# Seven block products instead of eight in all four gate and up pairs of two feed-forward stages

## What is computed

```python
def swiglu(x, w_gate, w_up, w_down):
    return (jax.nn.silu(x @ w_gate) * (x @ w_up)) @ w_down

    h = h + 0.5 * rmsnorm_2(swiglu(u, ff1_w_gate[i], ff1_w_up[i], ff1_w_down[i]), ff1_post_g[i])
    ...
    h = h + 0.5 * rmsnorm_2(swiglu(u, ff2_w_gate[i], ff2_w_up[i], ff2_w_down[i]), ff2_post_g[i])
```

## Time and profile before

| | us |
|---|---|
| median of 3 runs | 2850.26 |
| the runs | 2849.7 to 2850.55 |
| the profiled execution | 2850.18 |
| its span, first to last instruction | 2848.4 |
| mean granted TensorE clock | 0.998 |

### The profile page before, as it was taken

The page is one execution under the profiler, slowest core; times in us unless marked ns, Lnnn a source line. Parts: engine busy times, 40 slices in busy tenths (PEclk is TensorE's granted clock), DMA queues, the critical chain, the costliest instruction groups (busy, mean ns, idle before and its releaser), DMA issues.

```text
span 2848.4 us, 33903 instructions
## 1 busy us (share of the span) xinstructions
PE 2821.0 (99%) x13298; PEld 2358.2 (83%) x13298; DVE 2001.3 (70%) x2140; ACT 1379.1 (48%) x1544; POOL 14.4 (1%) x20
## 2 busy tenths in 40 slices
PE   9999999999999999999999999999999999999998
PEld 7888888888898788888888888888778888888887
DVE  5469756455565777777777777786777777777785
ACT  5344545454544544444444455655544444444464
POOL 0000000000000000000000000000000000000000
PEclk9999999999999999999999999999999999999999
DMA  7556355555546555555555558543655655555554
GB/s 239 194 165 197 111 186 180 193 180 176 168 148 201 187 197 189 195 195 195 198 192 191 192 170 270 173 151 129 221 178 188 206 191 191 194 195 197 195 177 155
DMA packets 276001, 530.60 MB, mean 186 GB/s; under 512 B 8769, under 2 KB 32465, under 8 KB 275393
## 3 DMA queue, kind: packets, MB, share of 16 engines
q1 hardware_dynamic: 274864, 527.01, 55.7%
q0 software_dynamic: 752, 2.04, 0.2%
q10 hardware_dynamic: 288, 0.20, 0.0%
HBM read 527.12 MB, written 2.10 MB: 186 GB/s over the span
## 4 chain that ended last, share of the span: by engine, by line
PE 91%; DVE 5%; ACT 2%; DMA 1%; issue 1%; SPq 0%; DVEq 0%; ACTq 0%
PE ps L760 23%; PE ps L761 23%; PE ps L763 21%; PE ps L1258 5%; PE ps L1259 5%; PE ps L1260 5%; PE ps L769 1%; DVE w_lo L2242 1%; ACT w_hi L1540 1%; PE ps L788 1%; PE ps L789 1%; PE ps L966 1%; PE ps L793 1%; PE ps L1252 1%; PE ps L946 1%
## 5 line engine op out<-in xcount | busy, mean ns | idle before, releaser
L2242 DVE TENSOR_TENSOR w_lo<-raw,w_hi 128x2048 fp32r<-128x2048 f32 (+3 forms) x398 | 883.6, 2227 | 351.9 <-ACT w_hi L1540 351.2
L760 PE MATMUL ps<-w_hi,x_hi 128*128 128x512 f32 (+3 forms) x2528 | 978.1, 387 | 3.0 <-ACT x_hi L1719 1.3
L761 PE MATMUL ps<-w_lo,x_hi 128*128 128x512 f32 (+3 forms) x2528 | 968.7, 383 | 0.0
L1540 ACT ACTIVATE w_hi<-raw 128x2048 fp32r<-128x2048 f32 (+3 forms) x398 | 738.3, 1864 | 340.0 <-DMA raw<-in_w_in 137.2
L763 PE MATMUL ps<-w_hi,x_lo 128*128 128x512 f32 (+4 forms) x2304 | 881.4, 383 | 0.0
L760 PEld LDWEIGHTS ps<-w_hi,x_hi 128*128 128x128 f32 x2528 | 475.3, 188 | 93.9 <-issue 1.7
L761 PEld LDWEIGHTS ps<-w_lo,x_hi 128*128 128x128 f32 x2528 | 475.5, 188 | 88.4
L763 PEld LDWEIGHTS ps<-w_hi,x_lo 128*128 128x128 f32 x2304 | 432.6, 188 | 83.2
L760 PE MATMUL ps<-w_hi,h_hi 128*128 128x512 f32 x640 | 249.2, 389 | 0.0
L763 PE MATMUL ps<-w_hi,h_lo 128*128 128x512 f32 x640 | 249.0, 389 | 0.0
L761 PE MATMUL ps<-w_lo,h_hi 128*128 128x512 f32 x640 | 249.0, 389 | 0.0
(11 more groups left out here) (413 smaller groups left out, 2876.7 us busy)
## 6 DMA issues: line engine op xcount, KB each, us to landing
raw<-in_w_in SPq DMA_DIRECT2D x139, 1024.0 KB, 5.0
raw<-in_ff_w_gate SPq DMA_DIRECT2D x88, 1024.0 KB, 5.2
raw<-in_ff_w_up SPq DMA_DIRECT2D x88, 1024.0 KB, 5.2
raw<-in_ff_w_down SPq DMA_DIRECT2D x88, 1024.0 KB, 5.1
raw<-in_w_out SPq DMA_DIRECT2D x45, 1024.0 KB, 5.1
raw<-in_w_ple_gate SPq DMA_DIRECT2D x16, 1024.0 KB, 5.0
raw<-in_w_in SPq DMA_DIRECT2D x8, 696.0 KB, 4.4
raw<-in_w_in SPq DMA_DIRECT2D x8, 520.0 KB, 3.7
```

The lines of the kernel that those rows point to most:

```text
L760: nc.tensor.matmul(o, x[0][:, k0 + c, s], hi[:, c, 0:width], start=first and c == 0, stop=False)
L761: nc.tensor.matmul(o, x[0][:, k0 + c, s], lo[:, c, 0:width], start=False, stop=False)
L1540: nc.scalar.activation(landed_part(w_hi, u, j), landed_part(raw, u, j), ACT.Copy).then_inc(hi_ready, 1)
L2242: V.tensor_tensor(landed_part(w_lo, u, j), landed_part(raw, u, j), landed_part(w_hi, u, j).bitcast(F32), ALU.subtract).then_inc(parts_read ...
```

## The change

`SUMMED = [0, 1, 2, 3]`: all four pairs are summed pairs. Pairs p1 and p3 were plain. With it:

- `summed_pair` has another order. Before: plain gate half, plain up half, the products with `w`, then those with `ws`. Now: plain gate half, plain up half, `ws` (9 matmuls), then the products with `w` (12), so that the slots of the pair are given free at the pair's end. In p3 the plain up half (12 matmuls) comes last.
- The shared products are complete only in p3: `rests` stands behind p3's splits, and ACT copies bank 6 when the gate products of p3 are done, beside p3's plain up half. A semaphore `shared_done` tells that bank 7 is done.
- In the loop the down products take banks 6 and 7 first, then 4 and 5 (`down_bank`), so down unit 0 waits for two of the four additions of `rests` and unit 1 for all.
- `turn_hidden` writes banks 6 and 7. The wait for the last `down_added` moves ahead, from behind the plain up half of p0 to in front of it.
- DVE and ACT make the `ws` parts before the halves of chunks 0 and 1, and the last `down_added` stands behind `sums_lo` instead of behind `pair_lo`.
- `x_sums` works on 4 pairs (512 columns) instead of 2 (256), and the rounding and the rests of `xs` come in three pieces. In `first_product` the activation comes before `sums_lo` and `pair_lo`.
- `xs_hi` lies where a gain row is loaded for the last stage. That load (4 transfers on POOL) waits for the last activation of the second feed-forward stage.

The diff, cut to its core:

```diff
+    SUMMED = [0, 1, 2, 3]
+    NS = len(SUMMED)
...
+        def down_bank(i, j):
+
+            return 4 + 2 * (j % 2 if isinstance(i, int) else (j + 1) % 2)
...
             nc.gpsimd.memset(out2, 0.0).then_inc(added, 1)
+            pool.wait_ge(hid_ready, 2 * FB)
...
                     if between:
                         between()
-                    pe.wait_ge(plain_ready, n * 2 + 2)
-                    for c in (2, 3):
-                        for tt in range(NT):
-                            three(tt, x(c, tt), of(up, c), start=q == 0 and c == 2)
-                    if before_rest:
-                        before_rest()
-                    first, last = q == 0, q == 1
-                    pe.wait_ge(parts_ready, u + 1)
-                    three(6, x(0, 0), of(gate, 0), first, last)
-                    three(2, x(1, 0), of(gate, 1)).then_inc(parts_used, 1)
-                    pe.wait_ge(parts_ready, u + 2)
-                    three(0, xsum(3), of(up, 1))
-                    three(7, xsum(2), of(up, 0), first, last).then_inc(parts_used, 1)
-                    if before_4:
-                        before_4()
+                    if p < 3:
+                        pe.wait_ge(plain_ready, n * 2 + 2)
+                        plain(0, up)
                     pe.wait_ge(ws_ready, n * 2 + 1)
                     three(4, xsum(0), sums(0), first, last)
                     three(5, xsum(1), sums(1), first, last)
                     pe.wait_ge(ws_ready, n * 2 + 2)
-                    three(3, x(1, 1), sums(2)).then_inc(ws_used, 1)
+                    three(3, x(1, 1), sums(2), False, p == 3).then_inc(ws_used, 1)
+                    if before_rest:
+                        before_rest()
+                    pe.wait_ge(parts_ready, u + 1)
+                    three(6, x(0, 0), of(gate, 0), first, last)
+                    three(2, x(1, 0), of(gate, 1), False, p == 3).then_inc(parts_used, 1)
+                    pe.wait_ge(parts_ready, u + 2)
+                    m = three(7, xsum(2), of(up, 0), first, last)
+                    if last:
+                        m.then_inc(shared_done, 1)
+                    m = three(0, xsum(3), of(up, 1))
+                    if p == 3:
+                        pe.wait_ge(plain_ready, n * 2 + 2)
+                        m = plain(0, up)
+                    m.then_inc(parts_used, 1)
 
                 def down(u, i, last=None):
-                    pe.wait_ge(rest_done, i + (no * (FB - 1) + 1))
                     for j in range(4):
+                        if j == 0:
+                            pe.wait_ge(rest_summed, i * 2 + (no * 2 * (FB - 1) + 2))
+                        if j == (0 if isinstance(i, int) else 1):
+                            pe.wait_ge(rest_done, i + (no * (FB - 1) + 1))
...
-                    act.wait_ge(ws_used, i * 2 + (n0 + 2))
+                    act.wait_ge(parts_used, u + (2 * SUMMED[-1] + 1))
                     nc.scalar.activation(gate_rest[:, 0], ps[:, 6, :], ACT.Copy).then_inc(p1_copied, 1)
...
-                    splits(u + 2, 2, 2)
-                    pair_plain_lo(0, n)
-                    pair_sums(0, n)
-                    pair_lo(u + 4, 0, n)
-                    sums_lo(n)
-                    splits(u + 6, 2, 2)
+                    for p in range(1, 4):
+                        j = 2 * p % RAW
+                        if p in SUMMED:
+                            n = i * NS + (n0 + SUMMED.index(p))
+                            pair_plain_lo(j, n, (0, 1) if p < 3 else (0,))
+                            pair_sums(j, n)
+                            sums_lo(n)
+                            pair_lo(u + 2 * p, j, n)
+                            if p == 3:
+                                pair_plain_lo(j, n, (1,))
...
                     rests(i)
                     splits(u + 8, 0, 2)
                     summed_product(u, i)
...
                     down_added(u + 8, i, 2)
                     pair_sums(0, n)
+                    sums_lo(n)
+                    down_added(u + 8, i, 3)
                     pair_lo(u + 12, 0, n)
-                    down_added(u + 8, i, 3)
                     hidden_lo(i + 1)
-                    sums_lo(n)
```

## The result

The changed kernel takes 2861.7 us (median of 6 runs, 2859.0 to 2864.0) where the kernel before, on the same chip, takes 2849.5 (2848.4 to 2850.6). The ratio is 1.0042, with a 95% interval of 1.0029 to 1.0055: slower by 12 us. The forecast was 2863.

A forecast was written before the change was run, and what follows sets the result against it. PE was taken as the bound, busy 2821 of 2848 us. The sum was 2850.2 - 27.2 + 38 + 1.1 + 1 = 2863 us; forecast 2857 to 2869 (60%), range 2850 to 2883.

The forecast's parts named there:

- 120 matmuls less: In p1 and p3, 6 matmuls fewer per turn over 20 turns, each 0.227 us: 27.2 us gained.
- stop at down unit 0: Before the down product PE waits 1.79 us for DVE's split behind four additions; with restart 1.9 per turn, 38 us.
- the written-out last block: The `summed_product` chain to down unit 2 comes 0.55 us late there, twice: 1.1 us.
- places without spare: Three places, among them down unit 2 and p0's wait for the last `down_added`: 1 us over both stages.
- the starts of the stages: Larger `x_sums` and more pieces cost about 4.7 us, the earlier activation returns 4.0: 0, within 2 us per stage.
- No spare, no loss: At down unit 2 and p0's wait for the last `down_added`, DVE's chain ends about when PE needs it.
- p3's `ws_lo`, 0.2 us to spare: In p3, DVE has `ws_lo` ready at 12.7 us after p1's end; PE comes to it at 12.9.
- DVE's work: Two more summed pairs add 9.1 us per turn, giving DVE 57.6 us of work in a turn of 63.5.
- The hidden chain: Rival: DVE reaches the split of down unit 0 in time, nothing else in the loop is late: 2825 us, 13%.
- DVE falls behind: Rival: DVE is late at several places in the loop, 0.4 to 1 us more per turn: 2870 to 2883, 10%.
- The clock falls: Rival: PE's clock drops to 1.2 GHz at each of 20 stops, about 1.5 us each: 2893 us, 5%.

The follow-up runs named there:

- experiment 1: Changed kernel with ACT's rounding and DVE's split of down unit 0 moved ahead of ACT's copy and the four additions: 2844.0 us, ratio 0.9981.
- experiment 3: Changed kernel plus a fifth 128x512 addition on DVE, result unused, between the third and the fourth: 2892.5 us, ratio 1.0147.
- experiment 2: Changed kernel with DVE's third and fourth addition of the shared products moved behind the split of down unit 0: 2866.6 us, ratio 1.0061.
- experiment 7: Changed kernel with a stage's first activation again behind `sums_lo` and `pair_lo`, as before the change: 2872.0 us, ratio 1.0077.
- experiment 5: Changed kernel with `SUMMED = [0, 1, 2]`, so that p3 is plain again: 2829.8 us, ratio 0.993.
- experiment 6: Changed kernel with `SUMMED = [0, 2]`, the same pairs summed as before the change but in the new order: 2838.4 us, ratio 0.9957.
- experiment 4: Experiment 1 plus DVE's split of down unit 2 and first down addition ahead of the activation, ACT rounding unit 2 before the tanh: 2821.7 us, ratio 0.9905.
- experiment 8: Experiment 4 plus the fifth 128x512 addition on DVE, result unused: 2825.4 us, ratio 0.991.
- experiment 10: Changed kernel plus a fifth addition on DVE of half the size, 128x256, result unused: 2882.1 us, ratio 1.0113.
- experiment 9: Experiment 4 with `x_sums` behind the activation's first step, its rests behind the last, and plain halves rounded first: 2818.5 us, ratio 0.9894.

## Why the prediction was right, point by point

The forecast was +12.8 us on the profiled execution, the trace has +12.7. That the sum agrees this closely is luck; the two terms that decide it, the matmuls and the stop, agree by themselves to 1.2 us, and the errors of the rest, up to 2.4 us, cancel:

| step | forecast | in the trace |
|---|---|---|
| 120 matmuls less | -27.2 | 120 less, -27.2 |
| stop at down unit 0, with restart, 20 times | +38 | 1.84 each, +36.8 |
| the written-out last block | +1.1 | about +0.6 |
| places without spare, and the rest of the loop | +1 | +3.4, of which 1.5 at down unit 2 |
| the starts of the stages | 0 | -0.3 |
| ahead of the first stage | not spoken of | -1.6 |
| behind the last turns | not spoken of | +1, not located |

- **Matmuls.** A summed pair is 45 matmuls of 0.227 us; the earlier trace rows carried this.
- **The stop.** Its parts as counted from the 27th matmul's start: copy at 0.43, first addition at 1.06, fourth at 3.11 in both. The split was taken at 3.75 and came at 3.71, PE's start at 6.10 and came at 6.04. This is where the forecast was made, and experiment 1 shows that the reason, too, is the right one: with the split (and its rounding) ahead of the additions, the stop is gone, and in experiment 3 one addition more lengthens it by the whole of that addition. The prediction has the unit rounded at 2.9 on this count, 0.85 ahead of the split, and does not call it a second limit; experiment 2 ran into it. The Trainium skill ("TensorE: Matmul & The Clock Gate", Architectural detail: the array is 16x 32x32, not 1x 128x128) says that VectorE's queue is strictly first in, first out; experiments 1 and 2 agree, since the split and the additions changed places only where the program did.
- **The last block.** PE's row before down unit 2 and the one behind it:

```profile
1618.17 0.39 PE L778 MATMUL ps<-w_hi,h_lo 128*128 128x512 f32 x1
1618.70 0.50 PE L775 MATMUL ps<-w_hi,h_hi 128*128 128x512 f32 x1
```

  0.53 from start to start, 0.30 late where 0.55 was forecast. The chain that decides it was the right one: it became the main wait in experiment 1.
- **No spare, no loss.** No wait stands at these places in the view of waits. Yet a turn is 0.13 us (first stage) and 0.24 us (second) longer than 64.83 - 1.36 + 1.84 = 65.31. Over 18 turns that is 3.4 us. In the second stage 1.5 of them are at down unit 2, the first of the three places: PE waits there in each turn, by so little that the row has no bracket.

```profile
2193.88 0.39 PE L778 MATMUL ps<-w_hi,h_lo 128*128 128x512 f32 x1
2194.16 0.49 PE L775 MATMUL ps<-w_hi,h_hi 128*128 128x512 f32 x1
2194.49 0.40 PE L776 MATMUL ps<-w_lo,h_hi 128*128 128x512 f32 x1
```

  From start to start 0.28 and 0.33 us instead of 0.227 twice: 0.05 of lateness and 0.10 of restart. In the first stage PE does not stop there. The other 1.9 us have no place that I can name.
- **p3's `ws_lo`, 0.2 us to spare.** It never became a wait.
- **DVE's work.** Forecast 57.6 us of a turn, measured 57.86.
- **The starts.** Each takes 2.2 us more to the summed product: 1.87 for its later place, and 1.84 - 1.36 for the first turn's stop and saving, which leaves -0.15. The zero is right, but it is the sum of two things of 4 us per stage (experiment 7). The prediction has both, 4.7 and 4.0; the expectations of experiments 5 and 6 forgot them, and came out 5 and 10 us too high: with smaller `x_sums` the gain of "activation first" is left over.
- **The hidden chain (13%).** It did not come. Its time, 2825, is reached only with another order (experiment 4, 2821.7).
- **DVE falls behind (10%).** Experiments 4 and 8 speak against it as a mechanism: 58.4 of 63.5 us of work, and no wait.
- **The clock falls (5%).** At the stops of the loop it did not, but the argument was too thin. One wait of 1.71 us without a drop was set against stops of 1.8; the changed kernel's are 1.57 to 1.67 by the bracket, and experiment 10 shows drops at 1.9. The margin was 0.3 us at most. With the error that I allowed for the stop itself, 5% was too low a chance.

## What to carry to other kernels

When work is taken away from an engine that is always busy, look for the pieces that stood between the last producer of a side chain and its consumer: count them in the busy engine's time, and set against them the chain in the side engine's own program order. Here that was 18 matmuls (4.1 us) against a chain of 6 us, and it cost more than the whole saving. Moving one piece in the queue moves the stop to the chain's next deadline (experiments 1, 2 and 9); what helped was to shorten the chain up to every deadline (experiment 4), and only then is the saving there. Two edits that cancel each other ("activation first" and the larger `x_sums`) have to be priced each by itself, and both prices carried into every variant that has only one of them.

## What the runs showed of the hardware

- **The clock.** I had not expected so narrow a margin: a stop of PE of 1.57 us in each turn left the granted clock at 1.00 in all 18 turns read (and in the 18 of experiment 7), 1.9 us let it fall to the 1.2 GHz level in 9 of 18, 2.2 us in 12 of 18. Each fall cost 1.5 us more, nearly as much as the stop. The same stops do not always end alike. At the start of a stage PE waits twice, 1.3 or 1.6 us and, 5 us later, 2.0; in the seven traces with this pair (the changed kernel, experiments 1 to 4, 8 and 10) the clock fell at 10 of 14 starts, so two kernels can differ by 3 us for this alone. Behind a single wait of 2.0 us (experiment 5) it fell at neither; two cases are too few to say that the first wait matters. The first stage of the changed kernel:

```profile
970.92 0.50 PE L1273 MATMUL ps<-w_hi,x_hi 128*128 128x512 f32 x1 [1.29 <-DVE w_lo L2973]
...
975.99 1.09 PE L1267 MATMUL ps<-ident,z 128*128 128x128 f32 x8 [2.03 <-DVE z L3041]
```
```profile
977.00:978.00 1.00, 1.00 (x4) 0.81 (x3) 1.00 (x2) 1.00 (x3) 0.00 (x0) 0.50 0.00 0
981.00:982.00 1.00, 1.00 (x6) 0.81 (x5) 1.00 (x2) 0.00 (x0) 0.00 (x0) 1.00 0.00 0
```
- **The restart** behind a wait costs 0.1 us beyond the wait, wherever it was read (0.31 to 0.34 us to the next start instead of 0.227). With 20 to 40 waits it is a term of its own (experiment 2).
